# A mixture of experts on one core: which experts are loaded first, and how their tokens are listed

## What is computed

```python
def hier_moe(h, w_group, b_group, w_router, b_router, w1, w3, w2):
    g_logits = (h @ w_group) + b_group              # 4 groups
    _, g_idx = lax.top_k(g_logits, 1)               # each token goes to one group
    g_w = softmax(g_logits)[g_idx]
    e_logits = ((h @ w_router) + b_router).reshape(t, 4, 8)
    top_v, top_i = lax.top_k(e_logits[its group], 2)  # and to two of its 8 experts
    weights = g_w * softmax(top_v)
    experts = g_idx * 8 + top_i
    ...
    expert(x, e) = (silu(x @ w1[e]) * (x @ w3[e])) @ w2[e]
    ...
    return sum over the token's two experts of weight * expert(token)
```

## Time and profile before

| | |
|---|---|
| time, median of 3 runs | 3447.9 us (3446.75 to 3449.11) |
| the profiled execution | 3446.33 us, span 3444.5 us |
| PE / DVE / ACT / POOL busy | 2907.5 / 1047.9 / 756.7 / 512.3 us |
| bytes read from HBM | 653.89 MB |
| mean granted PE clock | 0.942 of full speed |
| layer 0: routing starts / first unit's first product / last unit's silu | 596.96 / 643.64 / 1109.11 us |
| layer 0: first fixed expert's load issued / next phase's first load | 598.76 / 1118.97 us |
| layer 1: routing starts / first unit turned / last unit's silu | 1576.76 / 1615.78 / 2089.29 us |
| layer 1: first fixed expert's load issued / next phase's first load | 1578.57 / 2106.51 us |

### The profile page before, as it was taken

How to read it: one execution, slowest core, us unless ns; L and a number is a source line. 1 busy time by engine, 2 the same in 40 slices (tenths; PEclk the granted TensorE clock), 3 DMA queues, 4 the chain that set the end, 5 groups by cost and what they waited for, 6 DMA issues and landing times. The chain is left out here.

```text
span 3444.5 us, 50705 instructions
## 1 busy us (share of the span) xinstructions
PE 2907.5 (84%) x20913; PEld 1623.6 (47%) x20913; DVE 1047.9 (30%) x2201; ACT 756.7 (22%) x1483; POOL 512.3 (15%) x632
## 2 busy tenths in 40 slices
PE   7998888678776698895866663999999999999999
PEld 4555654355444345653543332444444554544444
DVE  3425856311111444754111113443211231211101
ACT  2224641111111323620111112311112220200000
POOL 0003630233323002511322220000000000000000
PEclk8999999799999899997988886999999999999999
DMA  7833022999997642026899996112222122322237
GB/s 296 312 135 115 1 92 93 398 426 426 426 425 304 220 113 96 1 110 256 367 423 423 424 423 239 58 50 82 73 73 73 49 74 83 82 86 80 98 119 259
DMA packets 188525, 679.10 MB, mean 197 GB/s; under 512 B 52766, under 2 KB 94222, under 8 KB 163782
## 3 DMA queue, kind: packets, MB, share of 16 engines
q1 hardware_dynamic: 176550, 655.66, 49.0%
q0 software_dynamic: 11808, 21.03, 1.6%
HBM read 653.89 MB, written 33.98 MB: 200 GB/s over the span
## 5 line engine op out<-in xcount | busy, mean ns | idle before, releaser
L1677 PE MATMUL pH<-w,room 128*32 128x256 f32 x5504 | 340.0, 401 | 77.5 <-DMA w<-in_moe_w 77.5
L2744 PE MATMUL banks<-hT,wf 128*128 128x512 f32 (+2 forms) x768 | 303.2, 557 | 3.3 <-ACT hT L2801 2.9
L1677 PEld LDWEIGHTS pH<-w,room 128*32 128x32 f32 x5504 | 217.7, 116 | 184.7 <-issue 110.9
L1713 DVE TENSOR_TENSOR hh<-hs,pH 128x128 f32<-128x128 f32 x118 | 33.9, 287 | 794.0 <-ACT hs L1696 794.0
L929 POOL TENSOR_SCALAR E<-E,st 128x768 f32<-128x768 f32 (+3 forms) x80 | 168.0, 2100 | 661.3 <-DVE st L1179 660.7
L1684 PE MATMUL pY<-w,hT 128*32 128x256 f32 x2752 | 166.3, 381 | 107.9 <-DVE hT L1715 103.5
L2744 PEld LDWEIGHTS banks<-hT,wf 128*128 128x128 f32 x768 | 140.8, 190 | 164.6 <-issue 154.9
L416 PE MATMUL pa<-aT,w 128*128 128x512 f32 x416 | 205.7, 599 | 1.3 <-DVE aT L680 1.3
L1677 PE MATMUL pH<-room 128*32 128x256 f32 x2048 | 136.1, 424 | 57.7 <-DMA room<-in_moe_w 34.8
L1684 PEld LDWEIGHTS pY<-w,hT 128*32 128x32 f32 x2752 | 96.4, 109 | 177.8 <-issue 134.3
L2490 PE MATMUL pa<-hT,ring 128*128 128x512 f32 x384 | 167.8, 592 | 0.0
(11 more groups left out here) (483 smaller groups left out, 3957.8 us busy)
## 6 DMA issues: line engine op xcount, KB each, us to landing
w<-in_moe_w SPq DMA_DIRECT2D x144, 2048.0 KB
room<-in_moe_w SPq DMA_DIRECT2D x48, 2048.0 KB
mw<-in_mod_w SPq DMA_DIRECT2D x24, 2048.0 KB, 16.6
ring<-in_w_ff_down SPq DMA_DIRECT2D x33, 1024.0 KB, 4.8
ring<-in_w_in SPq DMA_DIRECT2D x15, 2048.0 KB, 8.2
ring<-in_w_gate SPq DMA_DIRECT2D x6, 2048.0 KB, 8.7
wf<-in_w_ff_gate SPq DMA_DIRECT2D x11, 1024.0 KB, 5.6
wf<-in_w_ff_up SPq DMA_DIRECT2D x11, 1024.0 KB, 8.0
```

Of the source, the lines that this page charges most:

```text
L1677: last = pe.matmul(pH[strip(s), 0:2 * P].rearrange("p (j n) -> p j n", j=2), xT[:, k, :], slot_of(g, "w13", b)[:, :, k, s * P:(s + 1) * P] ...
L2744: last = pe.matmul(banks[f % 2][:, j * 512 + cols.start:j * 512 + cols.stop], wf[:, i % 2, j, k, (f % 2) * P:(f % 2 + 1) * P], hT[:, k, co ...
```

## The change

Five edits, all in the routing and expert phases:

1. The fixed positions hold experts 0, 8, 16 and 24, one of each group, in place of 0 to 3. `tie` gets more steps on POOL, since the bonus now goes to the multiples of 8.
2. The quarters come in another order (largest, third, second backwards, smallest), and each quarter begins with its last two ranks (`LATER = 2`), so that its own order starts two places later. POOL fills them in eight instructions in place of four.
3. The rounds of the row lists are done for four token tiles at once, with broadcast operands and a buffer for every tile; the third column block of `vals` is gone, and the row number alone tells which choice it was (two more instructions on the table). Four tiles (`count`, `place_of`, `down`, `table`) lie in memory lent by the first slot where it fits.
4. DVE turns the gated values in two halves, and PE waits for each half ahead of the products that read it.
5. POOL's loop runs one pair less; behind it come a drain, a clearing of the step semaphore and the last pair written out. The loop count for it is two more small DVE instructions.

```diff
...
 SLOTS = 4
+LATER = 2
 EARLY = {"w13": 4, "w2": 3}
...
...
         tmp2 = rest.sb(ph, "tmp2", [P, 2, nt, NE])
-        vals = ph.sb("vals", [P, 2, nt, 3, NU])
+        vals = ph.sb("vals", [P, 2, nt, 2, NU])
         m = ph.sb("m", [P, nt, 12])
...
...
         integer = ph.sb("integer", [P, 2, nt], I32)
-        slot = ph.sb("slot", [P, 2, P])
-        count, token = ph.sb("count", [P, P]), ph.sb("token", [P, NTILE])
-        place_of = ph.sb("place_of", [P, P])
+        slot = ph.sb("slot", [P, 2 * nt, P])
+        row_of = ph.sb("row_of", [P, 2, nt])
+        count, token = rest.sb(ph, "count", [P, P]), ph.sb("token", [P, NTILE])
+        place_of = rest.sb(ph, "place_of", [P, P])
         strip = ph.sb("strip", [P, 1])
-        down = ph.sb("down", [P, P])
+        down = rest.sb(ph, "down", [P, P])
         ones, earlier = ph.sb("ones", [P, P]), ph.sb("earlier", [P, P])
...
         by_count, need, begin = ph.sb("by_count", [NE, 1]), ph.sb("need", [NE, 1]), ph.sb("begin", [NE, 1])
+        group = ph.sb("group", [NE, NE + 1])
         listing = ph.sb("listing", [NE, 3, NE])
...
         first = ph.sb("first", [P, NE])
-        table = ph.sb("table", [P, 3, NU])
+        table = rest.sb(ph, "table", [P, 3, NU])
         pR = ph.ps("pR", [P, nt + 2, NE])
...
         pF = ph.ps("pF", [P, NE])
-        pV = ph.ps("pV", [P, 3 * NU])
+        pV = ph.ps("pV", [P, 2 * NU])
         const_in, exp_in, exp_out, used, ranked, slotted, slot_used = (
...
...
             step(pool.tensor_copy(key[:, NE:NE + 1], token[0:NE, 0:1]))
-            step(pool.tensor_scalar(tie[:], key[:], -1.0, float(SLOTS), ALU.mult, ALU.add))
-            step(pool.tensor_scalar(tie[:], tie[:], 0.0, 2.0 ** 17, ALU.max, ALU.mult))
+            step(pool.tensor_scalar(tie[:], key[:], float(EPG), None, ALU.is_ge))
+            for e in range(2, NG):
+                step(pool.tensor_scalar(group[:], key[:], float(e * EPG), None, ALU.is_ge))
+                step(pool.tensor_tensor(tie[:], tie[:], group[:], ALU.add))
+            step(pool.tensor_scalar(group[:], tie[:], float(EPG), None, ALU.mult))
+            step(pool.tensor_tensor(group[:], key[:], group[:], ALU.subtract))
+            step(pool.tensor_scalar(group[:], group[:], 0.0, None, ALU.is_equal))
+            step(pool.tensor_scalar(tie[:], tie[:], -(2.0 ** 17), SLOTS * 2.0 ** 17, ALU.mult, ALU.add))
+            step(pool.tensor_tensor(tie[:], tie[:], group[:], ALU.mult))
             pool.tensor_tensor(tie[:], tie[:], key[:], ALU.subtract)
...
             quarters = rank_at[:, SLOTS:SLOTS + 4 * n].rearrange("p (j q) -> p q j", q=4)
-            for q, (sign, first_rank) in enumerate(((-1.0, 2 * n - 1), (1.0, 2 * n), (1.0, 0), (1.0, 3 * n))):
-                pool.tensor_scalar(quarters[:, q], count[0:NE, 0:n], sign, float(SLOTS + first_rank), ALU.mult, ALU.add).then_inc(tabled, 1)
+            for q, (sign, first_rank) in enumerate(((1.0, 0), (1.0, 2 * n), (-1.0, 2 * n - 1), (1.0, 3 * n))):
+                for w0, w1, j0 in ((0, LATER, n - LATER), (LATER, n, 0)):
+                    pool.tensor_scalar(quarters[:, q, w0:w1], count[0:NE, 0:w1 - w0], sign, float(SLOTS + first_rank + sign * j0),
+                                       ALU.mult, ALU.add).then_inc(tabled, 1)
...
                 sp.dma_start(dst[:], g[src]).then_inc(const_in, 16)
-            for e in range(1, SLOTS):
-                load_gate(sp, g, l, e, e)
-                if e < EARLY["w2"]:
-                    load_down(sp, g, l, e, e)
+            for i in range(1, SLOTS):
+                load_gate(sp, g, l, i, i * EPG)
+                if i < EARLY["w2"]:
+                    load_down(sp, g, l, i, i * EPG)
...
...
             for i in range(2 * nt):
-                k, t = i % 2, i // 2
-                pe.wait_ge(slotted, i + 1)
-                pe.matmul(pV[:, :], slot[:, k, :], vals[:, k, t].rearrange("p a w -> p (a w)"),
-                          start=(i == 0), stop=(i == 2 * nt - 1)).then_inc(slot_used, 1)
+                pe.wait_ge(slotted, i // 4 + 1)
+                last = pe.matmul(pV[:, :], slot[:, i, :], vals[:, i // nt, i % nt].rearrange("p a w -> p (a w)"), start=(i == 0), stop=(i == 2 * nt - 1))
+            last.then_inc(slot_used, 1)
...
...
             dve.memset(upto[:, 0], 0.0)
+            for k in range(2):
+                dve.tensor_scalar(row_of[:, k], token[:, 0:nt], float(k * T), None, ALU.add)
             dve.tensor_copy(iota_i[:, 0:P], count[:])
...
...
-            dve.wait_ge(tabled, 4)
+            dve.wait_ge(tabled, 8)
             step(dve.scalar_tensor_tensor(out=key[:], in0=counts, scalar=float(NE), in1=tie[:], op0=ALU.mult, op1=ALU.add))
...
...
             dve.tensor_scalar(unit_end[:, NE - 1:NE], unit_end[:, NE:NE + 1], 1, None, ALU.arith_shift_left)
+            step(dve.tensor_scalar(odd[:], unit_end[:, NE:NE + 1], -1.0, None, ALU.add))
+            dve.tensor_copy(unit_end[:, 2 * NE + 1:2 * NE + 2], odd[:])
             dve.wait_ge(spread, 1)
...
...
             step(dve.tensor_tensor(item[:], own[:], whole[:], ALU.add))
-            for i in range(2 * nt):
-                k, t = i % 2, i // 2
-                v = vals[:, k, t]
-                if i >= 2:
-                    dve.wait_ge(slot_used, i - 1)
-                dve.tensor_scalar(slot[:, k, :], place_of[:], place[:, k, t:t + 1], None, ALU.is_equal)
-                step(dve.tensor_scalar(v[:, 1, :], count[:, 0:NU], item[:, k, t:t + 1], None, ALU.is_equal))
-                dve.tensor_scalar(v[:, 0, :], v[:, 1, :], token[:, t:t + 1], None, ALU.mult)
-                dve.tensor_scalar(v[:, 2, :], v[:, 1, :], float(k * T), None, ALU.mult).then_inc(slotted, 1)
+            places, items, rows_at = (x[:].rearrange("p k t -> p (k t)") for x in (place, item, row_of))
+            at = vals[:].rearrange("p k t a w -> p (k t) a w")
+
+            def each(x, i, n):
+
+                return x[:, i:i + 4].rearrange("p (a o) -> p a o", o=1).broadcast_to([P, 4, n])
+
+            def all4(x, n):
+                return x[:, 0:n].rearrange("p (o n) -> p o n", o=1).broadcast_to([P, 4, n])
+
+            for i in range(0, 2 * nt, 4):
+                dve.tensor_tensor(slot[:, i:i + 4], all4(place_of, P), each(places, i, P), ALU.is_equal)
+                step(dve.tensor_tensor(at[:, i:i + 4, 1], all4(count, NU), each(items, i, NU), ALU.is_equal))
+                dve.tensor_tensor(at[:, i:i + 4, 0], at[:, i:i + 4, 1], each(rows_at, i, NU), ALU.mult).then_inc(slotted, 1)
             step(dve.memset(gather_at[:, NU:NU + 3], BIG))
-            dve.wait_ge(slot_used, 2 * nt)
-            step(dve.tensor_copy(table[:].rearrange("p a w -> p (a w)"), pV[:, :]))
-            dve.tensor_scalar(table[:, 1], table[:, 1], -float(BIG), float(BIG), ALU.mult, ALU.add)
-            step(dve.tensor_tensor(table[:, 2], table[:, 0], table[:, 2], ALU.add))
-            for j in (0, 2):
-                last = dve.scalar_tensor_tensor(out=table[:, j], in0=table[:, j], scalar=float(STRIPS), in1=table[:, 1], op0=ALU.mult, op1=ALU.add)
+            dve.wait_ge(slot_used, 1)
+            step(dve.tensor_copy(table[:, 1:3].rearrange("p a w -> p (a w)"), pV[:, :]))
+            dve.tensor_scalar(table[:, 2], table[:, 2], -float(BIG), float(BIG), ALU.mult, ALU.add)
+            step(dve.tensor_scalar(table[:, 0], table[:, 1], float(T), -float(T), ALU.is_ge, ALU.mult))
+            step(dve.tensor_tensor(table[:, 0], table[:, 0], table[:, 1], ALU.add))
+            for j in range(2):
+                last = dve.scalar_tensor_tensor(out=table[:, j], in0=table[:, j], scalar=float(STRIPS), in1=table[:, 2], op0=ALU.mult, op1=ALU.add)
             step(last)
             dve.tensor_scalar(gather_at[:, 0:NU], table[:, 0], strip[:], None, ALU.add)
-            step(dve.tensor_scalar(scatter_at[:, 0:NU], table[:, 2], strip[:], None, ALU.add))
+            step(dve.tensor_scalar(scatter_at[:, 0:NU], table[:, 1], strip[:], None, ALU.add))
...
...
         block = ph.block()
+        half = HC // 2
...
         def pairs_of(eng):
-            return eng.value_load(unit_end[0:1, NE:NE + 1], min_val=1, max_val=NU // 2)
+            return eng.value_load(unit_end[0:1, NE:NE + 1], min_val=NE // 2, max_val=NU // 2)
...
...
             for i in range(EARLY["w2"], SLOTS):
-                load_down(sp, g, l, i, i)
+                load_down(sp, g, l, i, i * EPG)
             for i in range(SLOTS, NE):
...
...
             gather(2, 0)
-            n = pairs_of(pool)
-            with pool.Fori(0, n) as p:
-                step.restart()
+            n = pool.value_load(unit_end[0:1, 2 * NE + 1:2 * NE + 2], min_val=NE // 2 - 1, max_val=NU // 2 - 1)
+
+            def pair(p):
                 for b in range(2):
...
...
                     scatter(b)
+
+            with pool.Fori(0, n) as p:
+                step.restart()
+                pair(p)
+            pool.drain()
+            step.restart()
+            pair(n)
             for b in range(2):
```

(12 more changed lines are left out.)

## The result

The changed kernel takes 3418.3 us, median of four runs (3414.3 to 3425.1), against 3447.3 before (3444.5 to 3449.1): a ratio of 0.992, 95% interval 0.990 to 0.994, a gain of 29 us by the medians and 27 by the ratio. Measured again beside 21 runs of before, it took 3421.7 us and had a ratio of 0.993 (0.992 to 0.995), 23 us. The profiled execution took 3421.4 us, 24.9 less than that of before.

A forecast was written before the change was run, and what follows sets the result against it. The weight queue was taken to bound both expert stages, so savings count only where it is empty or behind its last byte. Layer 0 -5.0, layer 1 -11.0, last pair 0: -16.0 us from 3447.9, so 3432 us, range 3422 to 3443.

The forecast's parts named there:

- 1, routing: Row-list rounds of four token tiles at once: net 4.0 us saved in layer 0 and 2.0 in layer 1.
- The rule on tensor_tensor: Routing compare on DVE: by the skill's rule alone, the three groups would lose 0.8 us instead of gaining.
- Rival D: Layer 0's first units: PE stays at its low clock, ten units giving 3467 us; chance 0.04.
- 2, fixed experts: Expert stages: layer 1 11.0 us shorter, routing's gain included; layer 0's last byte 1 to 1.5 us later.
- the gap of 8.8: Layer 1's weight queue, 1680 to 1700 us: 8.8 us empty before, claimed to go.
- both places named: Layer 0's weight queue: dry before about 697 and again before 717 us, taken as 2.4 and 2.8 us.
- 3, quarters: Layer 0's expert order: earns nothing by itself, pays for the new fixed experts; stage 5.0 us shorter in all.
- 4, halves: Transpose of gated values: 0.1 us a unit, only at head and tail, 0.2 to 0.4 us; nothing in the body.
- 5, the last pair: End of POOL's loop in both layers: peeling the pair, with a drain ahead, was taken to gain 0.
- The bound of -7.4: Peeled last pair: the most it could gain, 7.4 us, with layer 1's 9.31 us drain becoming 2.
- Rival B: End of layer 1's loop: peeled pair also cuts the 9.31 us drain to 2, giving 3425 us; chance 0.18.
- Rival C: Layer 0's gain lost: routing no shorter, or two 5 us dry stretches, or another expert order; 3442 us, chance 0.16.

The follow-up runs named there:

- no_peel: The changed kernel with the last pair back in POOL's loop, all else as changed: 3428.7 us, ratio 0.995 to before.
- peel_no_drain: The changed kernel without the drain ahead of the written-out last pair: 3432.0 us, ratio 0.996 to before.
- fixed_alone: The kernel before with only the fixed experts changed to 0, 8, 16, 24: 3447.1 us, ratio 1.001.
- fixed_quarters: The kernel before with the new fixed experts and the new order of the quarters: 3439.5 us, ratio 0.998.
- halves_alone: The kernel before with only the gated values turned in two halves: 3439.2 us, ratio 0.999.
- peel_alone: The kernel before with only the last pair outside POOL's loop, behind a drain: 3439.6 us, ratio 0.998.
- debt_4: The changed kernel with the last pair back in POOL's loop and four more indirect DMAs, writing nothing, ahead of each layer's loop: 3431.9 us, one run.
- debt_16: The changed kernel with the last pair back in POOL's loop and sixteen more indirect DMAs, writing nothing, ahead of each layer's loop: 3459.1 us, one run.
- drain_each_pair: The changed kernel with the last pair back in POOL's loop and a drain ending each turn of it: 3425.7 us, ratio 0.995 to before.

## Why the forecast was right and where it failed

**1, routing: right, by its terms.** Rounds 8.3 and 5.4 us (said: 8.4 and 5.5); first load to first turned unit 4.4 and 2.2 us shorter (4.0 and 2.0). PE sets the pace with passes of 0.27 us (24 in 6.5). The rule on tensor_tensor, from "VectorE: DVE Perf Modes" of the Trainium skill, did no harm: the 512-column compare took 0.685 us, against four of 0.285. Not in the sum: PE's first unit loses 0.8 us to its low clock in layer 0 and 1.0 in layer 1. Rival D named the low clock and took ten units for it; it was one, and the next one ran at the full clock (3.64 us).

**2, fixed experts: right.** Layer 1's stage is 11.2 us shorter (11.0), the gap of 8.8 is gone. In layer 0 the queue runs dry at both places named, for 1.8 and 2.0 us (2.4 and 2.8). That layer 1 fits to 0.2 us is in part luck: no_peel and peel_no_drain, with edits 1 to 4 as they are, shortened it by 13.0 each, and in after the first unit's passes took 1.2 to 1.6 us longer than in these two.

**3, quarters: right.** fixed_alone and fixed_quarters bear out that they save 13 us of what edit 1 costs in layer 0; that they earn nothing by themselves was not run. Stage 0: 4.8 us shorter (5.0).

**4, halves: mechanism right, size off.** 0.19 us a unit, not 0.10. A 64-column transpose takes 0.268 us, not the 0.30 extrapolated from 128 and 256 columns; the wait shrank by more than that explains, and the rest was not followed up. The place was off too: the forecast counted head and tail alone, 0.2 to 0.4 us, while halves_alone took 1.2 and 2.1 us off the stages. Units ahead of an empty stretch of the queue count as well, since they set when its next load goes out.

**5, the last pair: the step that failed.** "I take 0, because both loops have the same code and only one drain is long" is wrong: the exits gave 2.0 + 5.9 us (1.2 to 1.6 and 5.3 to 5.4 against the other kernels without such a drain), peel_alone 6 us by itself, and POOL's drain changed, which the prediction had named as a sign of being wrong. That two drains behind the same code differ was read as a sign that the loop isn't the cause; it is, through how many indirect DMAs had run since the last drain. 1.95 and 9.31 looked unlike because layer 0 had, by the drain's length, paid for 110 of its DMAs in its loop. The bound of -7.4 was too near as well, for it left 1.95 standing in both layers, where 0.39 is reached; only the late place of the drain in layer 1 keeps the gain at 7 to 8. Rival B, at 0.18, had it that the peeled pair takes the long drain away, without saying why. Rival C did not come: neither dry stretch of layer 0 is over 2.0 us, and the routing did get shorter. The page "GPSIMD Engine Reference" of the Trainium skill, section on instruction dispatch, speaks of about 6 us for the first call of freshly loaded code; the drains here grow with the number of DMAs, so that isn't what they are.

**The rest.** -16.0 of the sum is no_peel's 16 us in time; its stages alone are 5.2 and 13.0 shorter, 2 us more than that. With 6 for peel_alone, or 8 from the exits, it makes the 22 to 24 that the second measurement, its stages and its exits show. The 27 to 29 of the first measurement have some 5 us more, which no stage shows, and that stays open; medians of before alone lie between 3444 and 3447, and single runs spread over more than 10 us. Range and chances were drawn from the profile's terms alone and left too little for this.

## What to carry to other kernels

Find the empty stretches of the resource that bounds a stage before counting any saving: here 0.19 us on 118 units gave 3 to 5 us and not 22, while 4.4 us ahead of layer 0's first unit came through whole. When work of unequal size goes through a ring of buffers, the pieces that are fixed before sizes are known should be spread over kinds, and the next ones ordered so that no buffer is held long twice in a row. A wait at the end of a phase whose length differs between equal phases is a lead, not chance: look for what accumulated in front of it, and pay it under other work, early enough.

## What the runs showed of the hardware

- A drain of POOL behind indirect DMAs took 0.06 us plus 0.082 for each one issued since the last drain (4, 12, 32, 56, 113: 0.39, 1.04, 2.68, 4.64, 9.30 us), though all had landed. Those ahead of an extra wait for landed DMAs at the start of the loop did not count (debt_4 and debt_16: 8.97 us, the price of 109). Issued while a scatter was under way, the drain waited for its landing too: median 8.5 us under the full weight queue (drain_each_pair), with an end 0.5 to 1.3 us after the last packet.
- Ahead of the 114th indirect DMA without a drain POOL stood 3.17 us, and a drain later found only 23 to pay for. The place moved with the count in debt_4 and debt_16 (122nd and 134th, 3.16 us). What happens there wasn't tried further; that it clears 110 at once is worked out from the drain's length.
- A drain after every fourth indirect DMA cost nothing that shows in layer 1 (stage 498.1 us against 497.7), where the engine had slack, and 5 us in layer 0.
- The 64 passes of a stage's first unit took 4.9 to 6.6 us with much the same code ahead of them. The granted clock over them was 0.68 of full speed in no_peel's layer 1 (5.34 us) and 0.55 in after's (6.52 us); the same passes of after's next unit took 3.64 us.
